# Routing the sample tile four heads at once, merged one-hot steps, and a pace in the split of the expert rows

## The reference

```
q = (xb @ w_q).reshape(t, 8, 2, 64)
s = einsum('thpd,hpnd->thpn', q, sub_keys)
s1, i1 = top_k(s[:, :, 0], 16)
s2, i2 = top_k(s[:, :, 1], 16)
cand = s1[..., :, None] + s2[..., None, :]          # 256 sums
cidx = i1[..., :, None] * 128 + i2[..., None, :]
sc, sel = top_k(cand, 16)
idx = take_along_axis(cidx, sel)
g = softmax(sc)
hid = einsum('td,thkd->thk', xb, u_tab[idx])
return einsum('thk,thkd->td', g * gelu(hid), v_tab[idx])
```

## Time and profile before

| | us |
|---|---|
| median of 3 runs | 3440.01 (3436.83 to 3442.25) |
| the profiled execution, its own time | 3433.54 |
| its span | 3431.8 |
| PE busy | 2676.2 (78%), granted clock 0.888 |
| DVE busy | 2760.4 (80%) |
| ACT busy | 797.4 (23%) |
| POOL busy | 2296.1 (67%) |
| DMA | 1277.03 MB, mean 372 GB/s |

### The profile page before, as it was taken

The page is one execution under the profiler, slowest core; times in us unless marked ns, Lnnn a source line. Parts: engine busy times, 40 slices in busy tenths (PEclk is TensorE's granted clock), DMA queues, the critical chain, the costliest instruction groups (busy, mean ns, idle before and its releaser), DMA issues.

```text
span 3431.8 us, 27484 instructions
## 1 busy us (share of the span) xinstructions
PE 2676.2 (78%) x7344; PEld 1233.6 (36%) x7344; DVE 2760.4 (80%) x6506; ACT 797.4 (23%) x1426; POOL 2296.1 (67%) x2198
## 2 busy tenths in 40 slices
PE   7567769988777877877878789988878877666777
PEld 4424424554333323444422234453433323222222
DVE  1588896787899998789898987898899989777761
ACT  4104132662111104142010141663101012200012
POOL 0176666666667777667777677777767767677771
PEclk9788979999889988988999889999988998877788
DMA  6599999999999999999999999999999999999993
GB/s 245 204 392 412 403 354 362 337 317 346 331 330 409 402 410 412 413 403 392 409 409 409 389 402 374 407 367 374 409 374 388 404 408 397 412 393 385 391 401 110
DMA packets 330977, 1277.03 MB, mean 372 GB/s; under 512 B 38148, under 2 KB 39172, under 8 KB 323528
## 3 DMA queue, kind: packets, MB, share of 16 engines
q0 software_dynamic: 313344, 1140.99, 85.8%
q1 hardware_dynamic: 17480, 134.28, 9.8%
HBM read 1267.45 MB, written 6.82 MB: 371 GB/s over the span
## 4 chain that ended last, share of the span: by engine, by line
PE 28%; DVE 25%; DMA 20%; POOL 13%; issue 10%; ACT 3%; DVEq 0%; ACTq 0%; SPq 0%; POOLq 0%
DMA urows<-in_peer_u,idx 14%; DVE urows L1260 9%; PE bank L1512 8%; PE experts L1539 7%; POOL urows L873 6%; POOL vrows L873 6%; DMA vrows<-in_peer_v,idx 4%; PE bank L1522 3%; PE att_out L1512 3%; DVE h L1297 2%; DVE diag L1286 1%; DMA urows<-in_peer_u,idx_sam 1%; DVE work L1156 1%; PE att_out L1522 1%; DVE part L1222 1%
## 5 line engine op out<-in xcount | busy, mean ns | idle before, releaser
L1539 PE MATMUL experts<-vrows,diag 128*128 128x512 f32 (+1 forms) x2876 | 1516.6, 672 | 567.7 <-DVE diag L1286 288.6
L1260 DVE CUSTOM_DVE_ANT_0 urows<-urows,query 128x1024 f32<-128x1024 f32 x1088 | 1311.7, 1211 | 247.2 <-DMA urows<-in_peer_u,idx 211.9
L873 POOL DMA_INDIRECT urows<-in_peer_u,idx x1024 | 1096.8, 1071 | 580.2 <-issue 233.3
L873 POOL DMA_INDIRECT vrows<-in_peer_v,idx x1024 | 1069.2, 1044 | 425.2 <-issue 279.3
L1539 PEld LDWEIGHTS experts<-vrows,diag 128*128 128x128 f32 (+1 forms) x2876 | 555.8, 205 | 1411.5 <-issue 1034.0
L1297 DVE SCALAR_TENSOR_TENSOR h<-vrows,amount,h 128x1024 f32<-128x1024 f32 x369 | 472.6, 1281 | 0.0
L1512 PE MATMUL bank<-weights,xT 128*128 128x512 f32 (+1 forms) x928 | 422.3, 607 | 9.5 <-ACT xT L933 3.7
L1512 PEld LDWEIGHTS bank<-weights,xT 128*128 128x128 f32 (+1 forms) x928 | 161.1, 177 | 247.3 <-issue 236.8
L924 ACT ACTIVATE work<-bank 128x256 f32<-128x256 f32 (+2 forms) x74 | 31.1, 421 | 682.1 <-PE bank L1730 525.5
L1286 DVE TENSOR_TENSOR diag<-ident,amount 128x512 f32<-128x512 f32 x256 | 175.8, 687 | 2.4 <-DVE amount L1270 0.3
L1512 PE MATMUL att_out<-weights,xT 128*128 128x512 f32 (+1 forms) x352 | 163.2, 614 | 0.0
(11 more groups left out here) (189 smaller groups left out, 2456.6 us busy)
## 6 DMA issues: line engine op xcount, KB each, us to landing
weights<-in_w_in SPq DMA_DIRECT2D x25, 2048.0 KB, 10.5
weights<-in_w_out SPq DMA_DIRECT2D x10, 2048.0 KB, 10.4
weights<-in_w_peer_q SPq DMA_DIRECT2D x10, 2048.0 KB, 10.4
urows<-in_peer_u,idx POOLq DMA_INDIRECT x1024, 9.8
vrows<-in_peer_v,idx POOLq DMA_INDIRECT x1024, 9.8
weights<-in_w_ple_gate SPq DMA_DIRECT2D x8, 2048.0 KB, 10.5
weights<-in_w_ple SPq DMA_DIRECT2D x4, 1024.0 KB, 8.1
weights<-in_sub_keysT SPq DMA_DIRECT2D x5, 512.0 KB, 6.7
```

The lines of the kernel that those rows point to most:

```text
L873: pool.indirect_dma_start(out=rows[:, where, :], out_offset=None, in_=table, in_offset=bass.IndirectOffsetOnAxis(ap=index, axis=0))\
L1260: dve.tensor_tensor_reduce(row, row, query[:, :], 1.0, 0.0, ALU.mult, ALU.add, hid[:, j % 2, k:k + 1]).then_inc(dotted.sem, 1)
L1539: last = pe.matmul(experts[c][0:ROWS[t], :], diag[:, (4 * j + q) % ND, k % QUARTER, 0:ROWS[t]], vrows[:, n % NV, 512 * c:512 * c + 512], s ...
```

## The change

- The sample tile is routed in 2 units a layer, each with four heads (0, 2, 4, 6 and 1, 3, 5, 7) on 128 partitions. A query product of the sample is now copied by ACT into `apart`, a zeroed buffer in `mlp`, at the 32 columns of its quarter. `score` for the sample sums four products over four heads, so each quarter of the partitions gets its own head's scores. A new stage `blank` has DVE zero that buffer, 128x1024, once a layer; ACT's write of the sample's embedding product into the same buffer waits for the last sample score.
- `pack` moves ahead of the sample's first `score` and copies only `h` and `scales` (6 DMAs); indices and exponentials are written where the gathers and amounts read them.
- In `choice`, the pairs of 128x256 instructions become one of 128x512 each. The table is given per layer, so the layer's offset is gone, and the index is one instruction. The division by the softmax's sum moves from `choice` to the amounts, as a third operand; the product with the gate there is gone.
- `LOAD` of `choice` goes from 0.6 to 0.4, which moves what `beside` lays between the steps.
- `shares()` has a third term, `PACE` x 4 = 10 us for a quarter: DVE adds the fewest rows at which neither estimate exceeds 10, and only beyond that the two are balanced. 273 of the 1088 rows go to DVE.

The core of the diff (dropping of the row count `r`, semaphores and array preparation left out):

```diff
 def query_stages(l, g, heads=range(H)):
+    if SAMPLE in PASSES[l, g]:
+        return [("blank", l)] + [("pq", l, g, e) for e in heads]
     return [("pq", l, g, e) for e in heads]
+def units_of(t):
+    return 2 if t == SAMPLE else H
 def routing_stages(l, tiles, alone=0):
-    names = [(l, t, e) for t in tiles for e in range(H)]
+    names = [(l, t, e) for t in tiles for e in range(units_of(t))]
...
-        at = out.index(("choice", l, SAMPLE, H - 1, STEPS["choice"] - 1))
-        out.insert(at + 1, ("pack", l))
+        out.insert(out.index(("score", l, SAMPLE, 0)), ("pack", l))
...
-        "score": (0.5, 0), "halves": (0, 0.6), "sums": (0, 0.6), "choice": (0, 0.6),
+        "score": (0.5, 0), "halves": (0, 0.6), "sums": (0, 0.6), "choice": (0, 0.4),
...
+PACE = 2.5
...
             out[j, q] = min(range(most),
-                            key=lambda n: max(pe + PE_ROW * (QUARTER - n), dve + DVE_STEP * QUARTER + DVE_ROW * n))
+                            key=lambda n: max(pe + PE_ROW * (QUARTER - n), dve + DVE_STEP * QUARTER + DVE_ROW * n,
+                                              PACE * QUARTER))
...
                 elif s[0] == "pack":
-                    eng.wait_ge(*routed.after((l, SAMPLE, H - 1)))
-                    for b in range(4):
+                    eng.wait_ge(*scale_kept.after((l, SAMPLE)))
+                    if l:
+                        eng.wait_ge(*query_ready.after((l - 1, SAMPLE)))
+                    for b in range(1, 4):
                         lo, hi = 32 * b, 32 * b + 32
-                        eng.dma_start(idx_sam[lo:hi, :], idx[0:DEC, SAMPLE, lo:hi]).then_inc(packed, 16)
-                        eng.dma_start(gate_sam[lo:hi, :], gate[0:DEC, SAMPLE, lo:hi]).then_inc(packed, 16)
...
                 elif step == 1:
-                    for p in range(2):
-                        mark(dve.tensor_tensor(hot3[p], iota16[0:r, :].unsqueeze(1).to_broadcast(full),
-                                               pos2[0:r, p, :].unsqueeze(2).to_broadcast(full), ALU.is_equal))
+                    mark(dve.tensor_tensor(flat, iota16[:, :].unsqueeze(1).to_broadcast(both),
+                                           pos2[:, :, :].rearrange("p a n -> p (a n)").unsqueeze(2).to_broadcast(both),
+                                           ALU.is_equal))
...
-                    mark(dve.tensor_scalar(gate[0:r, t, at], ex[0:r, n % 2, :], esum[0:r, n % 2, 1:2], None, ALU.mult))
                     settle()
-                    mark(dve.tensor_scalar(part[0:r, 0, :], part[0:r, 0, :], float(NKEYS), float(l * EXPERTS),
-                                           ALU.mult, ALU.add))
-                    settle()
-                    dve.tensor_tensor(idx[0:r, t, at], part[0:r, 0, :], part[0:r, 1, :], ALU.add)\
+                    dve.scalar_tensor_tensor(out=chosen(t, e), in0=part[:, 0, :], scalar=float(NKEYS),
+                                             in1=part[:, 1, :], op0=ALU.mult, op1=ALU.add)\
                         .then_inc(routed.sem, 1)
...
-                dve.tensor_tensor(amount[:, j % 2, :], act_hid[:, j % 2, :],
-                                  gate_sam[:, at] if t == SAMPLE else gate[:, t, at], ALU.mult)\
+                dve.scalar_tensor_tensor(out=amount[:, j % 2, :], in0=act_hid[:, j % 2, :],
+                                         scalar=share[:, t, e:e + 1], in1=exps(t, e), op0=ALU.mult, op1=ALU.mult)\
                     .then_inc(amounts_done.sem, 1)
...
+                elif kind == "blank":
+                    l = s[1]
+                    dve.wait_ge(*products_done.after(("mixT", l, SAMPLE)))
+                    dve.wait_ge(va_out, 16 * (l + 1))
+                    dve.memset(mlp[:, 2, :], 0.0).then_inc(blanked, 1)
...
+                        for x in heads:
+                            queries = apart[:, x, :] if t == SAMPLE else peer_queries(l, pass_of(l, t), x, [t])
+                            last = pe.matmul(b[:, NKEYS * p:NKEYS * p + NKEYS], queries[lo:lo + DH, :],
+                                             subT[lo:lo + DH, x, :], start=(x == heads[0]), stop=(x == heads[-1]))
```

101 lines of the change are left out of this document (56 added, 45 removed).

## The result

The changed kernel takes 3424.89 us (median of 5 runs, 3421.91 to 3428.02) against 3440.01 (median of 5 runs beside them, 3436.83 to 3444.58): ratio 0.9956, 95% interval 0.9941 to 0.997. That is 15 us, 0.44%, faster. The forecast was 39 us: the direction was right and the time lies in the range, but the gain is 0.4 of what the sum gave.

A forecast was written before the change was run, and what follows sets the result against it. No engine was full overall: by stretch, DMA gathers, VectorE, TensorE projections or, late, GpSimd set the pace. Terms -3 - 18 - 11 - 10 + 3 = -39 us took the 3440.01 us median to 3401, range 3352 to 3436.

The forecast's parts named there:

- Start, -3: 0 to 400 us: 3 to 5 head-routing savings lie on the path before the first gathers, -3 us (0 to -6).
- VectorE-full stretches, -18: Three VectorE-full stretches: 22 heads at 0.65 us save 14 us; a similar tile around 1850 to 1950 saves 4.
- the rates foretold (380, 340, 375): Sign of being right: 400 to 500, 900 to 1000 and 2500 to 2600 us above 380, 340 and 375 GB/s.
- 3000 to 3300, -11: 3000 to 3300 us: all 114 rows go to TensorE, gathers shorten, DMA engines bind at 406 GB/s, -11 us.
- TensorE as a bound: Rival: in the last stretch and 2000 to 2400 TensorE becomes the bound, +50 us, 3490; chance of 3447 to 3495: 0.11.
- The rival that counted a blocked gather as the larger cost: GpSimd's pace decides nearly everywhere, each removed addition gives back 0.65 us, total 3357; chance, shared with all caps, 0.24.
- 1000 to 2000 and 2600 to 3000, -10: These stretches rise from 404 and 406 towards 409 GB/s as heads, additions and blocked gathers thin out, -10 us.
- 2000 to 2400, +3: 2000 to 2400 us: about 13 rows reach a nearly full TensorE, most fitting in gaps, +3 us (-8 to +20).
- 500 to 900 and the end, 0: 500 to 900 us and the last 131 us: rows and order nearly unchanged, 0 us.

The follow-up runs named there:

- e11: Changed kernel plus 21 idle sums on VectorE in items 5 to 7 and an unused column that puts gathered rows at a multiple of 512 bytes: 3404.45 us.
- e1: Kernel before with only the threshold (PACE) added to the split of rows: 3431.82 us, ratio 0.9974.
- e5: Changed kernel with the planner's estimate of a choice stage set back to 0.6: 3419.12 us, ratio 0.9939.
- e12: Kernel before with only the planner's estimate of a choice stage lowered from 0.6 to 0.4: 3451.35 us, ratio 1.0036.
- e2: Changed kernel without the threshold (PACE) in the split of rows: 3429.35 us, ratio 0.9966.
- e10: Changed kernel plus 52 idle sums on VectorE in items 17 to 29 and an unused column that puts gathered rows at a multiple of 512 bytes: 3384.78 us.
- e13: Changed kernel plus one unused column that puts the gathered rows at a multiple of 512 bytes, no idle work: 3373.89 us, ratio 0.9824.
- e14: Kernel before plus an unused 192-byte buffer that puts the gathered rows at a multiple of 512 bytes: 3402.18 us, ratio 0.9891.
- e7: Changed kernel plus idle VectorE multiply-adds, both inputs in SBUF, at even steps of items 60 to 66: 3423.16 us, ratio 0.9952.
- e8: Changed kernel plus idle VectorE multiply-adds, one input in PSUM, at even steps of items 60 to 66: 3428.06 us, ratio 0.9962.

## Why the prediction was off, point by point

1. *Start, -3.* The saving came: 0-3 takes 130 to 133 us in every kernel with the new routing and 133 to 136 with the old. But the term spoke of 0 to 400 us, and item 5 begins 6.4 us later than before: I stopped at the first gathers, and 3-5 lost 7.6.
2. *VectorE-full stretches, -18.* The mechanism was right, as e11 shows (26.2 us for 25.5), and for the three stretches so was the size, where the order is the same on both sides: 15 us from e1 to e5 and from e12 to e2, for the 14 of the sum, with 0.59 us a head where I took 0.65. In the changed kernel only 8.3 arrived. The new order takes back 2.5 in 14-16 and 4.0 in 47-50 (e12), and the threshold about 2.5 in 5-8 (e2, e3). The tile routed from 1850 to 1950 gave 1.5 (items 34 to 37) and not 4. Of the rates foretold (380, 340, 375) only the first came: 382, 328, 370.
3. *3000 to 3300, -11.* Right: 298.8 to 289.8 us, 409 GB/s, clock 0.94, the gathers near 0.945. TensorE as a bound fell here: with more rows the granted clock was higher, and with 228.5 us for 465 matmuls of L1563 from 3000 to 3300 a row costs 4 x 0.491 = 1.97 us, where the sum had 2.05. The rival that counted a blocked gather as the larger cost fell as well: gathers lost 31 and 17 ns in the mean, and outside the last stretch nothing came of it. Its price was too high too: in the kernel before, gathers that begin inside an addition were lengthened by 145 us in all, 0.39 us for each addition and not 0.65.
4. *1000 to 2000 and 2600 to 3000, -10.* Here the mechanism failed. 16-30 gave 0.2 and 50-60 2.0. I read 404 under 409 as a gap that VectorE's and GpSimd's delays had made. e10 (with aligned rows) shows that 63 us more on VectorE don't lower the rate, e13 and e14 show the same 623 us in 16-30 for both kernels, and e2, with 97 additions there instead of 65, and so more gathers blocked, takes no longer than the changed kernel (634.7 against 636.9). What moved the rate was where the rows start. What keeps the mean of the long stretch under the best of it (in e13 too, 414 under 420) no run shows.
5. *2000 to 2400, +3.* A loss came, 7.7 us in 43-47, but not for the reason given: in e1 the rows moved and nothing was lost, in e2 they did not and it was, and e12 puts the order in their place.
6. *500 to 900 and the end, 0.* 8-14 moved by +1.8 and the end by +1.1. The small number in 8-14 is partly luck: the new order takes 4.5 off it (e12), and from there to the changed kernel it grows by 6.3.

So the forecast -3 -18 -11 -10 +3 became, by stretch, -4.4 -8.3 -9.0 -2.2 +7.7, with -3.2 from 30-43 and +7.6 from 3-5 that the sum did not have: -11.8. The start, 8-14 and the end add 6.1, so the traces differ by 5.6; the medians differ by 15.

Two steps of the sum failed. One is point 4: it priced a rise to 409 GB/s at 10 us, and 2.2 came, since neither VectorE's time nor the blocked gathers set the pace there. The other is the order of stages, which I had put at nothing because it removes and adds no instruction: it costs the kernel before 12 us (e12; 95% interval 8 to 17) and the changed kernel perhaps 6 (against e5; the intervals of the two overlap). It holds most of the loss in 43-47, about half of that in 3-5, and most of what point 2 lacks. The parts do not add up exactly: the routing code was worth 13 us from e1 to e5 and 22 from e12 to e2.

## What to carry to other kernels

A rate that stays the same in several stretches may be a ceiling, and taking work from an engine under it bought next to nothing here: put idle work there first, and see whether anything moves. Then ask what makes the ceiling; here the start address of the buffer that gathers write was worth three times the whole change, so look at where each buffer lies modulo 256 bytes whenever a kernel allocates one more or one less, and compare versions only at equal places. And a number that merely reorders stages cost more here (12 us) than the merged instructions saved (5 us): change it in a run of its own, and compare the rest at the same order.

## What the runs showed of the hardware that I had not expected

- With gathers of 4096-byte rows into SBUF, 1100 to 1400 and 2600 to 3000 us ran at 406 to 412 GB/s when the rows start 64, 128 or 224 bytes over a multiple of 256, and at 417 to 420 when they start on one.
- A gather that GpSimd starts during a VectorE instruction with two SBUF inputs ended 0.81 us after that instruction in nearly all cases. In step it loses 0.14 us (e7: 1.08 instead of 0.94), out of step up to 0.9 (the 1.82 of the earlier trace rows). With one input in PSUM it loses nothing (e8: 0.94).
- TensorE's granted clock over 3000 to 3300 was 0.77 while it was 64% busy and 0.94 while it was 81% busy: of the two levels, 1.2 and 2.4 GHz, it spent more time at the lower one where it had less to do.
- The time to the first dot product scatters between executions of kernels that begin alike: 132 to 141 us with the new routing, 135 to 141 with the old.
